# One 4 MB unit of expert weights sent as 112 + 8 + 8 partitions, in pairs 4, 8 and 12 of a hybrid block with a mixture of experts

## The reference

```
logits = (hf @ router_w) + router_b
top_v, top_e = lax.top_k(logits, TOP_K)
top_w = jax.nn.softmax(top_v, axis=-1)
...
gu = xb @ w_gate_up[e] + b_gate_up[e]
gate = jnp.minimum(gu[:, 0::2], SWIGLU_LIMIT)
up = jnp.clip(gu[:, 1::2], -SWIGLU_LIMIT, SWIGLU_LIMIT)
glu = gate * jax.nn.sigmoid(gate * SWIGLU_ALPHA)
return ((up + 1.0) * glu) @ w_down[e] + b_down[e]
```

## Time and profile before

| what | value |
|---|---|
| time, median of 3 runs | 1134.5 us (1132.52 to 1134.54) |
| span of the profiled execution | 1133.3 us |
| PE busy | 1083.3 us, 96% of the span |
| DVE, ACT, POOL busy | 349.8, 223.0, 44.1 us |
| moved by DMA | 439.23 MB, mean 388 GB/s |
| SP's queue q1 | 436.71 MB, 91.9% of 16 engines' span |
| weights in units of 4 MB | 67 transfers (45 gate and up, 22 down) |

### The profile page before, as it was taken

One profiled execution on the slowest core, in us unless ns is written; L12 is line 12 of the kernel. 1 busy time (PEld: TensorE's weight loads), 2 busy tenths in 40 slices (PEclk: granted clock), 3 DMA queues, 4 the chain that ended last, 5 costly groups with the idle time before them and its releaser, 6 DMA issues.

```text
span 1133.3 us, 14617 instructions
## 1 busy us (share of the span) xinstructions
PE 1083.3 (96%) x6237; PEld 530.3 (47%) x6237; DVE 349.8 (31%) x688; ACT 223.0 (20%) x354; POOL 44.1 (4%) x37
## 2 busy tenths in 40 slices
PE   7999999999999999999999889899989898999897
PEld 7889888734343434434343334243433333343432
DVE  4994887422213122222222222121203021223113
ACT  6645773301010101010101010101000101010002
POOL 0392000000000000000000000000000000000000
PEclk9999999999999999999999999899999999999999
DMA  8545469999999999999999999999999999999993
GB/s 309 201 150 206 165 239 374 403 420 412 426 432 431 434 428 428 434 427 431 434 426 431 434 428 426 438 427 431 431 430 431 432 431 427 434 425 432 425 425 154
DMA packets 36805, 439.23 MB, mean 388 GB/s; under 512 B 3028, under 2 KB 5736, under 8 KB 20488
## 3 DMA queue, kind: packets, MB, share of 16 engines
q1 hardware_dynamic: 35488, 436.71, 91.9%
q10 hardware_dynamic: 1256, 1.60, 0.4%
HBM read 437.25 MB, written 1.05 MB: 387 GB/s over the span
## 4 chain that ended last, share of the span: by engine, by line
PE 71%; DMA 26%; DVE 2%; issue 1%; ACT 0%; DVEq 0%; SPq 0%
PE PS L1775 29%; DMA W<-in_w_gate_up_dram 22%; PE PS L1839 12%; PE PS L1750 4%; DMA W<-in_w_down_dram 3%; PE PS L1437 3%; PE PS L1730 3%; PE PS L1441 3%; PE PS L1444 3%; PE PS L1423 3%; PE PS L1820 2%; PE PS L1796 1%; PE PS L1403 1%; PE PS L1476 1%; PE PS L1859 1%
## 5 line engine op out<-in xcount | busy, mean ns | idle before, releaser
L1775 PE MATMUL PS<-W,M 128*64 128x512 f32 x2048 | 465.8, 607 | 29.6 <-DMA W<-in_w_gate_up_dram 21.0
L1775 PEld LDWEIGHTS PS<-W,M 128*64 128x64 f32 x2048 | 147.3, 139 | 318.0 <-issue 285.9
L1839 PE MATMUL PS<-W,M 128*64 128x512 f32 x1024 | 226.3, 594 | 5.5 <-DMA W<-in_w_down_dram 5.5
L1256 DVE TENSOR_SCALAR M<-PS 128x256 f32<-128x256 f32 x64 | 27.0, 422 | 533.0 <-PE PS L1775 533.0
L1839 PEld LDWEIGHTS PS<-W,M 128*64 128x64 f32 x1024 | 74.1, 137 | 143.9 <-issue 142.0
L838 ACT ACTIVATE M<-M 128x256 f32<-128x256 f32 x64 | 26.7, 417 | 505.9 <-DVE M L1256 505.9
L843 ACT COPY M<-PS 64x512 f32<-64x512 f32 x31 | 17.9, 578 | 265.5 <-PE PS L1839 265.5
L1270 DVE COPY M<-PS 128x512 f32<-128x512 f32 x32 | 22.1, 692 | 127.4 <-PE PS L1820 127.4
L1730 PE MATMUL PS<-M,X 128*128 128x128 f32 x480 | 57.6, 278 | 0.0
L1750 PE MATMUL PS<-M,SELT 128*128 128x512 f32 x120 | 55.5, 605 | 0.0
L1730 PEld LDWEIGHTS PS<-M,X 128*128 128x128 f32 x480 | 54.7, 192 | 1.0
(11 more groups left out here) (261 smaller groups left out, 813.2 us busy)
## 6 DMA issues: line engine op xcount, KB each, us to landing
W<-in_w_gate_up_dram SPq DMA_DIRECT2D x45, 4096.0 KB, 41.4
W<-in_w_down_dram SPq DMA_DIRECT2D x22, 4096.0 KB, 41.0
W<-in_w_gate_up_dram SPq DMA_DIRECT2D x38, 2048.0 KB, 15.7
W<-in_w_down_dram SPq DMA_DIRECT2D x17, 2048.0 KB, 17.2
W<-in_w_in_dram SPq DMA_DIRECT2D x10, 2048.0 KB, 8.0
W<-in_w_down_dram SPq DMA_DIRECT2D x5, 1024.0 KB, 44.0
W<-in_w_out_dram SPq DMA_DIRECT2D x2, 2048.0 KB, 10.6
W<-in_w_in_dram SPq DMA_DIRECT2D x2, 1024.0 KB, 9.5
```

What stands on the lines that cost most here:

```text
L1775: ins = mm(gu[half][64 * g:64 * g + 64, :], hTe[:, k, tok], gu_slot[slot][:, kk, c:c + 512], start=(k == 0), stop=(k == KD - 1))
L1839: ins = mm(dst[64 * n:64 * n + 64, :], actT[b][:, 4 * kh + k, :], dn_slot[slot][:, k, 512 * n:512 * n + 512], start=(kh == 0 and k == 0), ...
```

## The change

In pairs 4, 8 and 12 the unit m = 4 (the first half of gate and up of the second expert) is no longer one transfer of 128 partitions. SP issues one transfer of partitions 0 to 111, which counts on `slot_loaded[4]` as before, and then one of partitions 112 to 119 and one of 120 to 127, which both count on a new semaphore, `edge_loaded`. PE waits for both semaphores before its first matmul on this unit. The bytes, their places and everything else stay.

```diff
+UNEVEN = (4, 8, 12)
...
+        edge_loaded = sem("edge_loaded")
...
+            def load_uneven(e, j, m):
+
+                src, dst = unit_src(e, m), slots(ring(j, m), 2)
+                sp.dma_start(dst[0:112], src[0:112]).then_inc(slot_loaded[m], 16)
+                for p0 in (112, 120):
+                    sp.dma_start(dst[p0:p0 + 8], src[p0:p0 + 8]).then_inc(edge_loaded, 16)
...
-                        load_unit(e, j, m)
+                        if m == 4 and j in UNEVEN:
+                            load_uneven(e, j, m)
+                        else:
+                            load_unit(e, j, m)
...
                     pe.wait_ge(slot_loaded[m], r * (16 * PAIRS) + 16 * (j + 1))
+                    if isinstance(r, int) and m == 4 and j in UNEVEN:
+                        pe.wait_ge(edge_loaded, 32 * (UNEVEN.index(j) + 1))
```

## The result

The changed kernel takes 1207.8 us, the median of 4 runs (1201.7 to 1209.7), against 1134.1 us of the kernel before in the same comparison: a ratio of 1.0638, with a 95% interval from 1.0621 to 1.0654. That is 74 us more, 24.6 us for each of the three units. The forecast had the direction; 1207.8 lies outside its range.

A forecast was written before the change was run, and what follows sets the result against it. The DMA weight stream bounds the kernel. Three units cost eight engines +25.5 to +32.7 us, less 8 us of lead: +21 on 1133.3, 1154.4, plus 1.2 for the runs' median, said as 1156 us; range 1130.5 to 1172.

The forecast's parts named there:

- The bound: Whole kernel: the DMA stream of weights is the clock until 1078 us; time lost on the last-landing engines delays the end.
- the pace: Weight stream: 26.9 GB/s per engine, so a 32 KB row takes 1.22 us and a full unit 9.75 us.
- the issues: SP's queue: two more issues for each of three units, 0.33 us each, 2 us in all, costing nothing.
- The 112 rows: Wide transfer of each unit: seven rows per engine, no extra cost taken, at most 4 us per unit allowed.
- The narrow transfers: The two 8-row transfers: four or five engines share a group of four partitions, +8.5 to +10.9 us per unit.
- The lead of 8 us: End of the weights: eight engines finish some 8 us ahead; if they carry the narrow rows, 8 us is swallowed.
- The balance: Rows per engine: eight engines carry 9 rows of a unit, eight carry 7; 3.65 us for three units by count.
- only the count matters: Rival for the 8-row transfers: no crowding, engines landing last lose 3.65 us of work, 1130.9 us; chance 0.21.
- Mild crowding: Rival for the narrow rows: 6.3 us on all engines, less or plus 3.65, 1137.2 to 1144.5 us; chance 0.14.
- the small loads: 32-partition loads of b_gate_up and b_down: rates beside them of 345 and 338 GB/s, read as writers meeting.
- the 112 rows meet as well: Case for the wide transfer: its rows crowd too, up to 12 us above 1152 to 1159; chance 0.07.
- the last DMA stretch: Sign in the chain of waits: its last wait on a weight transfer ends near 1100 instead of 1078.5 us.

The follow-up runs named there:

- the run with four rows: Changed kernel, but in pairs 4, 8 and 12 only partitions 112 to 115 of the unit are sent, as one transfer: 1121.4 us.
- the control: Changed kernel, but the unit is cut by columns into three transfers of 128 partitions (7168, 512, 512 columns), same semaphores: 1134.7 us.
- the run made for it: Changed kernel, but each transfer is strewn: three sets of every fourth partition, the fourth set as 8, 8 and 16 rows: 1144.8 us.
- the 96: Changed kernel, but only partitions 0 to 95 of the unit are sent, side by side in one transfer: 1163.3 us.
- the 56 + 56 rows: Changed kernel, but partitions 0 to 111 go as 56 even, then 56 odd ones, the last 16 unsent: 1186.3 us.
- halves: Changed kernel, but the three units go as two transfers of 64 adjacent partitions each, no row left out: 1180.2 us.
- quarters: Changed kernel, but the three units go as four transfers of 32 adjacent partitions each: 1182.5 us.

## Why the prediction was wrong in its size

**The bound, the pace and the issues** were right. The stream is the clock (the chain leaves it 75.8 us later for a loss of 74), a row of 1.22 us gives the loss of the run with four rows to 0.4 us, and three transfers with a second semaphore cost nothing (the control, 1134.7 us).

**The 112 rows are the step that failed.** The prediction allowed "Below, nothing; above, I allow 4 us per unit", and then "I take nothing". They cost 12.1 us a unit with the last sixteen rows unsent, 13.3 over their own time at full pace, half of the whole loss. A larger price was at hand: its own bound from the earlier trace rows, 2.1 us for each 0.52 MB, gave 14.7 us for 3.67 MB, and was cut to 4 without a row that said so. Seven rows at half pace are 8.5 us more; some four rows behind them, also at half pace, would complete the 13.3.

**The narrow transfers** were put at +8.5 to +10.9 us a unit over full pace; measured are 11.4 by the windows, and 11.1 as the difference of two kernels (12.3, less the 1.2 us that sixteen rows take at full pace). The mechanism of the text, four or five engines to a group, gives the right size. Its scope was wrong: the text made eight engines late and left the other eight alone, and all sixteen slowed down.

**The lead of 8 us** therefore swallowed nothing. A lead is there between engines, and a stall of all of them doesn't use it; moreover the eight in question seem to hold two that trail. With three times 13.3 and 11.4 us on all engines and nothing taken off, the same sum gives 1134.1 + 74.1 = 1208.2 us. That the instruction queue makes this lead, as the prediction had it, no run tested.

**The balance**, 3.65 us by count, is neither shown nor excluded: some 2 us are left for it, by subtraction, in the run made for it, where crowding cost four times as much.

**The rivals.** That only the count matters, 1130.9 us, falls: with most of the crowding gone the time is 1144.8, and without the 8 us that are left of it, 1136.8, still not below the kernel before. Mild crowding, 2.1 us a unit, falls with the 11.4. Its source, the rate beside the small loads, rose when they were spread, but as much was lost right behind, so the earlier trace rows alone do not price crowding. The nearest was that "the 112 rows meet as well", at 0.07 and up to 12 us more; it had the place, and a third of the price. Of what the text had said one would see, the PE waits (+15 to +30) and the last DMA stretch (near 1100) came out at +75 and 1154.3, and the dips at 180 to 240 GB/s for some 40 us, not under 380 for 20. For the landing of the 256 KB transfers the view shows no time.

**What stays open.** The rows that each engine gets of a transfer that isn't the full 128 were not seen: no row of the trace names an engine or a partition. That two engines share a group all through the 112, the 96 and the 56 + 56 rows is inferred from the half pace and from its absence where a transfer of 32 or 64 rows is strewn over all 128 partitions. Why 64 even rows run at full pace and 56 do not is not explained. Nor is it shown why a second and third unit cost more than the first (17, 21, 25 us), and why only the wide part grows; engines that are already out of step would do it.

## What to carry to other kernels

Cut a large transfer by columns, or by every second or fourth partition over the whole height, not by ranges of partitions: columns and 64 + 64 strewn rows were free here, 64 + 64 adjacent rows cost 15 us for each 4 MB. Measure a stride with another number of rows first, as 56 + 56 strewn rows cost 17. Where a transfer is narrow by nature, price it at the engines that meet in one group of partitions, and charge that to every transfer in flight, since the whole core waits for it. And if a bound worked out from rows is uncomfortable, it stays in the range until a row excludes it.

## What the runs showed of the hardware

- One crowded group of partitions sets the pace of all sixteen DMA engines: 4 rows of 32 KB side by side, 128 KB, cost the core 4.5 us, and 15 us more in three units than the same rows spread.
- The pace falls to a half: 210 of 430 GB/s over 15 us in windows of 5, for halves and for quarters, with the engines' share at 0.96 to 1.02. A full DMA share says nothing of the rate.
- 96 rows as three sets of every fourth partition run at 413 to 452 GB/s, so full pace needs neither 128 rows nor one transfer.
- Spreading the small loads of the earlier trace rows raised the rate beside them by some 50 GB/s, but from 188 to 240 us as a whole it stayed (403 and 402 GB/s), and so did the time.
